# Two transformer blocks on one core: the attention steps of stages "a" and "n" taken two at a time

## The reference

```
sc = jnp.einsum('bqhd,bkhd->bhqk', qb, k).astype(jnp.float32) * scale
sc = jnp.where((key_pos[None, :] <= q_pos[:, None])[None, None], sc, NEG)
p = jax.nn.softmax(sc, axis=-1).astype(v.dtype)
return jnp.einsum('bhqk,bkhd->bqhd', p, v)
```

## Time and profile before

| | us |
|---|---|
| median of 3 runs (1533.56 to 1535.06) | 1534.08 |
| the profiled execution | 1537.27 |
| its span, first to last instruction | 1535.4 |
| TensorE busy in the span | 1485.4 |
| VectorE, ScalarE, GpSimd busy | 655.4, 620.4, 650.5 |

### The profile page before, as it was taken

One profiled execution on the slowest core, in us unless ns is written; L12 is line 12 of the kernel. 1 busy time (PEld: TensorE's weight loads), 2 busy tenths in 40 slices (PEclk: granted clock), 3 DMA queues, 4 the chain that ended last, 5 costly groups with the idle time before them and its releaser, 6 DMA issues.

```text
span 1535.4 us, 20810 instructions
## 1 busy us (share of the span) xinstructions
PE 1485.4 (97%) x7827; PEld 1223.6 (80%) x7827; DVE 655.4 (43%) x1381; ACT 620.4 (40%) x1119; POOL 650.5 (42%) x446
## 2 busy tenths in 40 slices
PE   7999999999889999999999989999999999999998
PEld 6888888677667888899897667777888888888886
DVE  4337958357453141421235566662132323332323
ACT  4453654466563222343234466773224222222222
POOL 4333645243332444434333355553444444444442
PEclk9999999999999999999999999999999999999999
DMA  5223432102001333446332200003222222222232
GB/s 185 90 78 91 143 97 81 53 20 82 29 1 55 97 97 96 151 121 188 118 90 69 65 18 2 1 2 133 99 98 83 96 96 96 96 96 96 96 97 94
DMA packets 72521, 130.44 MB, mean 85 GB/s; under 512 B 5799, under 2 KB 29426, under 8 KB 72434
## 3 DMA queue, kind: packets, MB, share of 16 engines
q1 hardware_dynamic: 71730, 127.09, 26.1%
q10 hardware_dynamic: 704, 2.17, 0.4%
HBM read 125.05 MB, written 4.19 MB: 84 GB/s over the span
## 4 chain that ended last, share of the span: by engine, by line
PE 91%; DVE 3%; ACT 3%; issue 2%; POOL 1%; DMA 0%; DVEq 0%; ACTq 0%; POOLq 0%
PE bank L817 71%; PE bank L1027 5%; PE bank L879 4%; PE bank L1019 4%; PE bank L768 3%; PE bank L881 1%; PE bank L1209 1%; PE bank L1064 0%; ACT w_hi L1413 0%; PE bank L1378 0%; DVE q_parts L2189 0%; POOL w_lo L651 0%; DVE proj L2659 0%; POOL sc L684 0%; DMA cst<-cst_d 0%
## 5 line engine op out<-in xcount | busy, mean ns | idle before, releaser
L651 POOL TENSOR_TENSOR w_lo<-raw,w_hi 128x1024 fp32r<-128x1024 f32 (+4 forms) x222 | 520.9, 2348 | 714.7 <-ACT w_hi L1413 714.5
L1413 ACT ACTIVATE w_hi<-raw 128x1024 fp32r<-128x1024 f32 (+4 forms) x222 | 226.5, 1022 | 612.0 <-DMA raw<-in_w_ff 254.8
L817 PE MATMUL bank<-w_hi,xt_hi 128*128 128x484 f32 (+2 forms) x640 | 240.1, 375 | 2.9 <-POOL w_lo L651 2.9
L817 PE MATMUL bank<-w_lo,xt_hi 128*128 128x484 f32 (+2 forms) x640 | 237.5, 371 | 0.0
L817 PE MATMUL bank<-w_hi,xt_lo 128*128 128x484 f32 (+2 forms) x640 | 237.4, 371 | 0.0
L817 PE MATMUL bank<-xt_hi,w_hi 128*128 128x512 f32 x576 | 227.9, 396 | 1.1 <-issue 1.1
L817 PE MATMUL bank<-xt_hi,w_lo 128*128 128x512 f32 x576 | 224.7, 390 | 0.0
L817 PE MATMUL bank<-xt_lo,w_hi 128*128 128x512 f32 x576 | 224.6, 390 | 0.0
L817 PEld LDWEIGHTS bank<-w_hi,xt_hi 128*128 128x128 f32 x640 | 120.6, 188 | 18.6 <-issue 3.9
L817 PEld LDWEIGHTS bank<-w_hi,xt_lo 128*128 128x128 f32 x640 | 120.6, 188 | 15.0
L817 PEld LDWEIGHTS bank<-w_lo,xt_hi 128*128 128x128 f32 x640 | 120.7, 189 | 14.2
(11 more groups left out here) (349 smaller groups left out, 2343.3 us busy)
## 6 DMA issues: line engine op xcount, KB each, us to landing
raw<-in_w_ff SPq DMA_DIRECT2D x64, 512.0 KB, 3.5
raw<-in_w_in SPq DMA_DIRECT2D x40, 512.0 KB, 3.4
raw<-in_w_in SPq DMA_DIRECT2D x40, 484.0 KB, 3.4
raw<-in_w_in SPq DMA_DIRECT2D x24, 392.0 KB, 3.2
raw<-in_w_out SPq DMA_DIRECT2D x16, 512.0 KB, 3.5
raw<-in_w_branch SPq DMA_DIRECT2D x12, 512.0 KB, 3.6
raw<-in_w_mem_kv SPq DMA_DIRECT2D x8, 512.0 KB, 3.6
raw<-in_w_proj_nsa SPq DMA_DIRECT2D x8, 512.0 KB, 3.4
```

Of the source, the lines that this page charges most:

```text
L651: pool.tensor_tensor(w_lo[:, slot, 0:halves, 0:width], raw[:, slot, 0:halves, 0:width], w_hi[:, slot, 0:halves, 0:width].bitcast(F32), ALU ...
L817: ins = pe.matmul(o, lhs, rhs, start=st and j == 0, stop=en and j == 2)
L1413: act.activation(w_hi[:, slot, 0:halves, 0:width], raw[:, slot, 0:halves, 0:width], ACT.Copy)\
```

## The change

In stages "a" and "n" the loop takes two places at a time. At an even place TensorE issues the transposes of `pos - 3` first and then the scores, and no V products; at an odd place the scores, the transposes of `pos - 3`, and then the V products of `pos - 5` and `pos - 4`. Over two places E and E+1 that is: transposes of E-3, scores of E, scores of E+1, transposes of E-2, V products of E-4 and E-3. At even places VectorE and ScalarE take their copy of turned probabilities ahead of masks and exponentials. In "n" there are 6 buffers for turned probabilities instead of 4. The number and kind of instructions stay the same.

```diff
+TOGETHER = "an"
...
-                more = [proj[:, t, W1C + S:W1C + 2 * S] for t in range(2)]
+                more = [proj[:, t, W1C + S:W1C + 2 * S] for t in range(4)]
...
+        def applied_at(stage, pos):
+            if stage not in TOGETHER:
+                both = (pos,)
+            else:
+                both = (pos - 1, pos) if pos % 2 else ()
+            return [p for p in (entry(stage, q) for q in both) if is_step(p)]
+
+        def turns_first(stage, pos):
+            return stage in TOGETHER and pos % 2 == 0
...
+            def turn_step(stage, pos):
+                p, sc_of, SC = entry(stage, pos), sc_slots(stage), SC_OF[stage]
+                if is_step(p):
+                    wait_copied(pe, 2 * p - 2)
+                    wait_copied(pe, 2 * p - 1)
+                    for u in (2 * p, 2 * p + 1):
+                        pe.wait_ge(sem["normed"], u + 1)
+                        turn(u, sc_of[u % SC])
...
+                    if turns_first(stage, pos):
+                        turn_step(stage, pos - LAG_T)
...
-                    p = entry(stage, pos - LAG_T)
-                    if is_step(p):
-                        wait_copied(pe, 2 * p - 2)
-                        wait_copied(pe, 2 * p - 1)
-                        for u in (2 * p, 2 * p + 1):
-                            pe.wait_ge(sem["normed"], u + 1)
-                            turn(u, sc_of[u % SC])
-                    p = entry(stage, pos - LAG_PV)
-                    if is_step(p):
+                    if not turns_first(stage, pos):
+                        turn_step(stage, pos - LAG_T)
+                    for p in applied_at(stage, pos - LAG_PV):
...
 # ScalarE; VectorE's loop likewise, ahead of the masks
+                    if turns_first(stage, pos):
+                        copy_turned(p)
                     if is_step(e):
                         exps(2 * e)
+                    if not turns_first(stage, pos):
+                        copy_turned(p)
```

More of the change, by code:

```diff
@@ L1065, in apply_compressed @@
                           start=False, stop=False, skip_group_check=True)
+            def turn_step(stage, pos):
[6 more added lines that the diff above has]
+                        turn(u, sc_of[u % SC])
             def attention(stage):
                 p0, p1 = pairs_in(stage)
-                sc_of, prob_of, SC = sc_slots(stage), prob_slots(stage), SC_OF[stage]
+                prob_of = prob_slots(stage)
                 LAG_T = LAG_T_OF[stage]
@@ L1673, in exps, with copy_turned @@
                                    accum_out=sums[:, u % SC:u % SC + 1]).then_inc(sem["exps"], 1)
[L1675 to L1678, removed]
+                def copy_turned(p):
                     if is_step(p):
@@ L1686, in attention @@
                            .then_inc(sem["copied_a"], 1)
+                for pos in range(len(ORDER[stage]) + LAG_T):
+                    e, p = entry(stage, pos), entry(stage, pos - LAG_T)
+                    if turns_first(stage, pos):
+                        copy_turned(p)
+                    if is_step(e):
+                        exps(2 * e)
+                    if not turns_first(stage, pos):
+                        copy_turned(p)
                     if e == "keys":
@@ L2290, in attention, with copy_turned @@
                 nsa = stage == "n"
+                def copy_turned(p):
+                    if is_step(p):
+                        u = 2 * p
+                        w = UNITS[u]
+                        dve.wait_ge(sem["probs_t"], u + 1)
+                        wait(dve, sem["applied"], u - len(prob_of) + 1)
+                        n, r = (w["n"], P) if w["n"] >= P else (P, w["n"])
+                        dve.tensor_copy(prob_of[u % len(prob_of)][0:r, 0:n], bank[2 + u % 2][0:r, 0:n])\
+                           .then_inc(sem["copied_d"], 1)
                 for pos in range(len(ORDER[stage]) + LAG_EMPTY):
@@ L2298, in attention @@
                         weigh(STRIP_M2 + 3, True, None, None, first_half=True)
+                    if turns_first(stage, pos):
+                        copy_turned(entry(stage, pos - LAG_T))
                     if e == "rows":
```

## The result

The changed kernel takes 1538.79 us (median of 7 runs, 1537.47 to 1541.34), the kernel before 1534.08 (7 runs of the same comparison, 1533.07 to 1535.06). The ratio is 1.0032, with a 95% interval of 1.002 to 1.0043: 4.7 us slower, where 5.4 was forecast (1539.5). One run of the kernel before, beside the experiments, took 1858.78 us at a mean granted clock of 0.753 and is left out of the ratios.

The account below looks back on a forecast made before the run. TensorE was taken as the bound, at 91% of the chain. Terms of 2.8 + 0.6 + 1.3 + 0.5 + 0.3 = 5.5 us on 1534.08 gave 1539.6, said as 1539.5; likeliest range 1537 to 1543, 8 in 10 1528 to 1547.

Parts of the forecast that it names:

- The forecast's own case: Whole kernel: new waits for copies outweigh the saved tile switches, 3 to 9 us slower; chance 0.50.
- Part 1: TensorE in "n": fewer trips to V's tiles, one more per pass for the compressed product; 9.7 us less, 1.2 per pass.
- Part 2: "n": transposes wait for late copies, 1.3 us in i = 2 and 0.45 in i = 3 blocks; net +2.8 us.
- The first pass, taken as 0: First pass of "n": set by VectorE's late gating and compressed work before and after; 0, bounds -2 and +2.
- Part 4: Stage "a": saved switches -2.7 us, new waits +2.3, entry and end +1.0; sum +0.6 us.
- Part 5: Compressed transposes in "n", two pairs: the second waits 0.85 us for ScalarE's copy instead of 0.2; +1.3 us.
- Part 6: End of "n": two transpose groups without scores between, +0.5 us; ScalarE's weight split in the second pass's i = 2 block, +0.3.
- Part 3: Prob buffers in "n", 4 to 6: copies there never wait for V; costs nothing.
- Part 7: Copies ahead of masks at even places: cost nothing; without them the block's second transposes would wait.
- Waits hidden: Rival: copies in i = 2 and 3 blocks end 1.0 us earlier, waits shrink to 0.3 per pass; 1528 us; chance 0.20.
- A wash: Rival: passes come out even at waits of 1.2 and only the ends cost; 1534 to 1537 us; chance 0.18.
- The clock falls: Rival: new waits in "n" lower the granted clock; 1545 us if in three passes, 1552 in every pass; chance 0.12.

Follow-up runs that it names:

- V pairs alone: Changed kernel with V products still in pairs, but at even places scores before transposes and copies behind masks and exponentials, as before the change: 1539.35 us, ratio 1.0035.

## Why the prediction was right, point by point

**The sign and the size.** 4.7 us where 5.4 was summed. The forecast's own case, two waits a pass that outweigh the saved switches, is what the trace shows and what the experiments with the copies and the emptying confirm: with the waits nearly removed the same work on TensorE is faster than before. That the sum came within 0.8 owes something to luck: terms that were too small (the pass) and too large (parts 5 and 6), and a saving that was not counted, cancel, and the first pass is even for another reason than the one given.

**Part 1, the switches: right.** TensorE's own work in a pass is 18.06 - 1.26 - 0.40 = 16.40 us; the forecast had 17.56 - 1.2 = 16.36. The trip of the compressed product is 0.35 in its experiment. The Trainium skill, TensorEngine Tiling (Array Packing), section "Tiling Modes", says that changing the tiling mode drains TensorE. Those 0.35 us agree with it, and by it alone the sign would have been wrong.

**Part 2, the waits: right in place and size.** 1.26 for 1.3 and 0.40 for 0.45. A pass gained 0.5 us and I had rounded that to 0.4: seven times, 3.5 for 2.8 (a pass of 18.06 us, where 17.9 was to show it). The forecast names VectorE's unbroken row in the i = 2 block; the two runs with the emptying and with ScalarE's copy alone show two floors close to each other, VectorE's (a wait of 1.08 without ScalarE's) and ScalarE's (0.84 without the emptying). Only with the copies of both engines ahead is it 0.24. The Trainium skill, TensorEngine Tiling (Array Packing), section "Performance Considerations", says that the copy out of PSUM may become the bottleneck once TensorE is sped up. The traces agree, but as an order of queues and not as a load: busy time of both engines in a pass is nearly the same with a wait of 1.25 as with one of 0.24 (11.82 and 12.42 us, 11.83 and 12.22).

**The first pass, taken as 0: the number held, by luck.** From the first scores of "n" to the end of its last V product it is 911.75 - 881.04 = 30.71 us, before 914.76 - 883.82 = 30.94. Within that, waits of 2.91, 1.42, 0.43 and 0.44 stand for ones of 1.37, 0.46 and 0.93 before, 2.4 more. What pays for them is the saved switches (1.2) and less time at a lower clock: before, the granted clock was 0.54 from 892.84 to 897.60 and 0.75 up to 902.60, after, 0.64 from 890.21 to 895.00 and 1.00 behind it, some 1.7 us less lost. The forecast had no such term.

**Passes 2 to 8.** To the end of the last V product they take 1044.23 - 911.75 = 132.48 us for 1043.97 - 914.76 = 129.21: +3.3. Before, a stretch at half clock lies in them that the changed kernel's profile hasn't: from the last V product at 954.40 to the next transposes it took 3.12 us, at full clock 1.84 (933.49 - 931.65 in the pass before). At like clock it is +4.6. The forecast's terms for these passes are 2.8 (part 2), 0.65 (one of the two pairs of part 5, the other is in the first pass) and 0.8 (part 6): 4.25.

**Part 4, stage "a": 0.6 was within what can't be told.** Its steady pass takes 8.53 us for 8.60, with the forecast wait (0.61 for 0.65), in TensorE's timeline:

```profile
299.67 0.63 PE L1032 MATMUL bank<-cst,sc 128*128 128x128 f32 x4 [2.58 <-ACT prob_t L1701]
...
309.37 0.63 PE L1032 MATMUL bank<-cst,sc 128*128 128x128 f32 x4
...
313.08 1.07 PE L1032 MATMUL bank<-cst,proj 128*128 128x128 f32 x8 [0.61 <-DVE prob_t L2324]
...
317.90 0.63 PE L1032 MATMUL bank<-cst,sc 128*128 128x128 f32 x4
```

The wait of 2.58 at the entry stands for 0.74 and 1.19 before. "a" ends at 332.39 us, and at 333.88, 333.14 and 332.22 in three profiles whose "a" is the old one, so a profile doesn't tell; the run with "n" alone says 0, give or take about 2.

**Part 5, near.** The second compressed transposes wait 0.44 and 0.64 us, where I had 0.85 each. ScalarE's copy ends where I placed it (they start 983.11 - 980.24 = 2.87 us into the block, 2.9 forecast), but TensorE gets there later, at 2.23 and in the other block at 2.43, for 2.1. From the last scores ahead of them to these transposes it is 0.72 and 0.92 us, before it was 0.26 in both: together 1.1 more, for 1.3. **Part 6:** the wait with the weight split is 1.77, 0.5 above the others, for 0.3, but that pass was 0.4 longer than the others before too (17.98 for 17.56), so that the change adds only 0.1 to it beyond the 0.5 of every pass; the end of "n" has a wait of 0.63 more than it had, for 0.5. The 1.92 near 953 is 1.44 now, which I had not counted (-0.5).

**Part 3:** buffers put at nothing, and nothing they cost; but going back to four costs 3.2 us by the median, 1.8 of it by the waits, which the forecast didn't say of "n". **Part 7: right, and the dearest of all.** Without it the change would be 24 us slower than before.

**The rivals.** *Waits hidden*: the trace doesn't meet its condition. The kernel with copies first nearly does (0.24 a pass) and takes 1532.2, where the rival had 1528; with the emptying and the compressed product moved too, which the rival didn't count on, it is 1530.6. *A wash* falls with the interval. *The clock falls*: not in the steady passes, at waits of 1.26; it did in four of seven at 1.98.

## What to carry to other kernels

Putting like tiles beside each other on TensorE saves what the switches cost, but it takes away the work behind which other engines' copies were done: before pairing, place each copy in its engine's queue against the moment at which TensorE comes back. An engine that is 30% idle can still make TensorE wait in every pass, and where two engines are late by nearly the same, taking away the lateness of one shows little. Reorder the copies together with the products: here that turned 4.7 us lost into 3.4 won (5.3 with "a" left alone).

## What the runs showed that I had not expected

Waits of 1.26 us in every pass left the granted clock at 1.00 in the steady passes; waits of 1.98 in seven passes were followed by the lower level behind four of them in the profile and not behind the other three, so that 0.72 more of waiting cost 9.0 us in all rather than 4.5. In between it is open: a wait of 1.43 or 1.44 us near 951, the same in eleven of the profiles, was followed by the lower level in four of them (0.52, 0.52, 0.53 and 0.65 over the next 3 us) and by full clock in seven. One such stretch cost 1.3 us in the run with four buffers, more than the price of some edits here, so single profiles have to be compared stretch by stretch.

And waits can hide in TensorE's own row. With V pairs alone a pass is 18.14 us, and that row shows 0.74 of waiting in it; the row of the weight loads shows 1.93, with the engine that was waited for.
